# Attention's first score and softmax units placed between the query projections of a two-block kernel

## The reference, cut to what matters

```python
z = rmsnorm(h, g_mix) @ w_in                       # zq: 512, zkv: 768, zg: 24, zc, zm
kc = gelu((kv[0] blocks of 32, stride 16, + pos) @ w_cmp_k1) @ w_cmp_k2   # 31 compressed keys
vc = gelu((kv[1] blocks + pos) @ w_cmp_v1) @ w_cmp_v2
o_c = softmax(q kc^T * 64**-0.5, causal by block end) @ vc        # compressed branch
o_s = softmax(q ks^T * 64**-0.5, causal) @ vs                     # selected: all 8 blocks here
o_w = softmax(q kw^T * 64**-0.5, causal in 512) @ vw              # window: all 512 keys here
o   = gates[0] * o_c + gates[1] * o_s + gates[2] * o_w            # gates = sigmoid(zg)
y_a = o @ w_o_nsa
c   = causal depthwise convolution of 31 taps over c_val * sigmoid(c_gate), 512 channels
```

## Time and profile before

| | us |
|---|---|
| median of 3 runs (2225.15 to 2229.15) | 2225.91 |
| the profiled execution | 2225.84 |
| its span | 2224.1 |
| PE busy in the span | 2059.4 (93%) |
| DVE, ACT, POOL busy | 934.8, 569.8, 349.7 |
| share of PE in the chain that ended last | 81% |

### The profile page before, as it was taken

The page is one execution under the profiler, slowest core; times in us unless marked ns, Lnnn a source line. Parts: engine busy times, 40 slices in busy tenths (PEclk is TensorE's granted clock), DMA queues, the critical chain, the costliest instruction groups (busy, mean ns, idle before and its releaser), DMA issues.

```text
span 2224.1 us, 23734 instructions
## 1 busy us (share of the span) xinstructions
PE 2059.4 (93%) x9948; PEld 1278.4 (57%) x9948; DVE 934.8 (42%) x1319; ACT 569.8 (26%) x879; POOL 349.7 (16%) x231
## 2 busy tenths in 40 slices
PE   5999999899888898988899889988999999999998
PEld 3888777443424233333324235764687778888877
DVE  3667574310101011111111104777786467777554
ACT  4534313100000000000000003337434343334453
POOL 2212021000000000000000001125533323225440
PEclk8999999899999999999999999998999999999998
DMA  8552116699999999999999992330222322232220
GB/s 284 198 201 102 39 51 253 263 390 419 428 427 427 428 428 428 427 428 428 428 427 427 428 424 106 73 104 10 75 77 80 119 76 94 96 111 70 104 95 38
DMA packets 107178, 529.06 MB, mean 238 GB/s; under 512 B 14925, under 2 KB 43713, under 8 KB 82241
## 3 DMA queue, kind: packets, MB, share of 16 engines
q1 hardware_dynamic: 107073, 527.55, 59.4%
HBM read 525.43 MB, written 2.10 MB: 237 GB/s over the span
## 4 chain that ended last, share of the span: by engine, by line
PE 81%; DVE 6%; DMA 6%; issue 3%; ACT 2%; POOL 1%; SPq 0%; ACTq 0%; DVEq 0%
PE bank L992 21%; PE bank L598 13%; PE bank L599 13%; PE bank L600 13%; PE bank L1043 6%; DMA f<-in_w_gate_dram 5%; PE bank L953 3%; PE bank L966 3%; PE bank L609 2%; DVE f L2338 1%; PE bank L852 1%; PE bank L1234 1%; PE bank L1202 1%; PE bank L798 1%; DVE r L383 1%
## 5 line engine op out<-in xcount | busy, mean ns | idle before, releaser
L992 PE MATMUL bank<-f,high 128*64 128x512 f32 x2048 | 472.0, 607 | 49.8 <-issue 31.5
L390 POOL TENSOR_TENSOR r<-f,r 128x1024 fp32r<-128x1024 f32 (+3 forms) x86 | 231.2, 2708 | 1600.9 <-ACT r L377 1564.6
L598 PE MATMUL bank<-r 128*128 128x512 f32 (+1 forms) x1016 | 404.9, 398 | 15.6 <-DVE r L1935 5.0
L599 PE MATMUL bank<-r 128*128 128x512 f32 (+1 forms) x1016 | 399.5, 393 | 0.0
L600 PE MATMUL bank<-r 128*128 128x512 f32 (+1 forms) x1016 | 398.9, 393 | 0.0
L992 PEld LDWEIGHTS bank<-f,high 128*64 128x64 f32 x2048 | 152.2, 139 | 339.5 <-issue 324.8
L2262 DVE SCALAR_TENSOR_TENSOR f<-bank,low,f 128x512 f32<-128x512 f32 x64 | 48.0, 750 | 507.1 <-PE bank L966 507.1
L1043 PE MATMUL bank<-f,high 128*64 128x512 f32 x1024 | 228.8, 604 | 17.4 <-issue 17.4
L598 PEld LDWEIGHTS bank<-r 128*128 128x128 f32 (+1 forms) x1016 | 191.5, 188 | 70.1 <-issue 19.0
L1413 ACT ACTIVATE high<-bank 128x512 f32<-128x512 f32 (+2 forms) x93 | 51.5, 583 | 676.5 <-PE bank L609 340.7
L599 PEld LDWEIGHTS bank<-r 128*128 128x128 f32 (+1 forms) x1016 | 191.9, 189 | 42.4 <-issue 1.7
(11 more groups left out here) (357 smaller groups left out, 1972.2 us busy)
## 6 DMA issues: line engine op xcount, KB each, us to landing
f<-in_w_down_dram SPq DMA_DIRECT2D x66, 2048.0 KB, 21.4
f<-in_w_up_dram SPq DMA_DIRECT2D x64, 2048.0 KB, 22.0
f<-in_w_gate_dram SPq DMA_DIRECT2D x63, 2048.0 KB, 21.6
f<-in_w_in_dram SPq DMA_DIRECT2D x14, 2048.0 KB, 7.9
f<-in_w_up_dram SPq DMA_DIRECT2D x22, 1024.0 KB, 7.1
high<-in_w_ada_dram SPq DMA_DIRECT2D x32, 512.0 KB, 5.4
f<-in_w_ada_dram SPq DMA_DIRECT2D x4, 2048.0 KB, 17.5
f<-in_w_out_dram SPq DMA_DIRECT2D x4, 2048.0 KB, 8.0
```

The costliest lines, as they stand in the source:

```text
L390: up(g.tensor_tensor(low_part(c)[:, z], whole(c)[:, z], high_part(c)[:, z].bitcast(F32), ALU.subtract), "lo_g", c, i)
L598: pe.matmul(o, wh, xh, start=first, stop=False)
L599: pe.matmul(o, wl, xh, start=False, stop=False)
L992: ins = pe.matmul(o[64 * e:64 * e + 64, :], xsT[p % 2][:, 2 * k + r, 64 * e:64 * e + 64], ws[e](2048 * r + 512 * fc), start=k == 0 and r = ...
```

## The change

**Buffers.** Units 0 and 1 write their scores to `PS_first`, two stretches that the projections have used up: the first lies over the column temporaries `ct` and over `pcs`, the second over the spent rows `kcat`. Units 2 to 7 keep `PS[un % 4]`.

**First part.** On PE the scores of unit 0 follow the second query projection, those of unit 1 the third, those of unit 2 the fourth; `hidden_rows` comes behind them. The turn of banks 2 to 7 starts two projections earlier, so the third and fourth projections go to banks of that turn, 2 and 3. ACT's copies of the queries stand between the exponentials. DVE does 39 taps ahead of the first `scored` (55 before), and 4, 4 and 2 among the first three units.

**Compressed branch.** `hidden_turned` and `second_layer` move into unit 0, `compressed` into unit 1 and `compressed_turned` into unit 2.

**Steady part.** On ACT `exps(un + 2, 0)` and `exps(un + 2, 1)` in step un become `exps(un + 2, 1)`, after `turned(un, 0)`, and `exps(un + 3, 0)`, at the end of the step, ahead of the division of `w_o_nsa` and `high_output`. Taps: none in step 1, as before in 2 to 4, 7 instead of 4 in each of 5 to 7; 42 are left behind attention (41 before).

```diff
+        PS_first = [mem(2560, M + 24704), mem(2560, M + 12928)]
...
+        def scored_at(un):
+            return PS_first[un] if un < 2 else PS[un % 4]
...
             for i in range(4):
                 o = take(("q2", i), "a_z", "q2", i)
                 up(project(o[:, :], Q2, i, U2H, U2L), "pe_z", "q2", i)
                 if i == 0:
                     to_tokens(1, 128)
                     to_tokens(2, 24)
+                else:
+                    if i == 1:
+                        turn["order"], turn["i"] = [2, 3, 4, 5, 6, 7], 0
+                        pe.wait_ge(s["v_z"], val("v_z", "kz", 1))
+                    pe.wait_ge(s["a_z"], val("a_z", "q2", i // 2))
+                    for n in range(3):
+                        scores(i - 1, n)
...
-            pe.wait_ge(s["a_z"], val("a_z", "q2", 3))
-            pe.wait_ge(s["v_z"], val("v_z", "kz", 1))
-            for un in range(2):
-                for n in range(3):
-                    scores(un, n)
             hidden_rows()
-            for n in range(3):
-                scores(2, n)
-            hidden_turned()
-            second_layer()
-            compressed()
             for un in range(8):
                 turned(un, 0)
+                if un == 0:
+                    hidden_turned()
+                    pe.wait_ge(s["a_z"], val("a_z", "q2", 3))
+                if un == 1:
+                    compressed()
                 if un < 5:
                     scores(un + 3, 0)
                 turned(un, 1)
+                if un == 0:
+                    second_layer()
+                if un == 2:
+                    compressed_turned()
                 if un < 5:
                     scores(un + 3, 1)
-                if un == 1:
-                    compressed_turned()
...
+            queries(0)
+            a.wait_ge(s["v_z"], val("v_z", "tk", 2))
+            up(a.activation(flat(GT), flat(GT), ACT.Sigmoid), "a_z", "gt")
+            queries(1)
             exps(0, 0)
+            queries(2)
             exps(0, 1)
+            exps(1, 0)
+            queries(3)
+            exps(1, 1)
+            exps(2, 0)
             a.wait_ge(s["pe_cmp"], val("pe_cmp", "rows"))
             up(a.activation(hrow, bank("cm")[:, 0:256], ACT.Gelu_apprx_tanh), "a_cmp", "rows")
-            exps(1, 0)
-            a.wait_ge(s["pe_cmp"], val("pe_cmp", "hid"))
-            up(copy(HID.rearrange("p h w g n -> p (h w g n)"), bank("cmT")[:, 0:256]), "a_cmp", "hid")
-            exps(1, 1)
             for un in range(8):
                 turned(un, 0)
+                if un == 0:
+                    a.wait_ge(s["pe_cmp"], val("pe_cmp", "hid"))
+                    up(copy(HID.rearrange("p h w g n -> p (h w g n)"), bank("cmT")[:, 0:256]), "a_cmp", "hid")
                 if un < 6:
-                    exps(un + 2, 0)
-                if un == 0:
+                    exps(un + 2, 1)
+                if un == 1:
                     a.wait_ge(s["v_att"], val("v_att", "pcs"))
                     up(a.activation(flat(pcs), flat(pcs), ACT.Exp), "a_att", "pc")
                 turned(un, 1)
-                if un < 6:
-                    exps(un + 2, 1)
-                if un == 1:
+                if un == 2:
                     a.wait_ge(s["pe_att"], val("pe_att", "pcT", 0))
                     up(copy(pcT[:, 0, :], bank("pcT", 0)[:, :]), "a_att", "pcT", 0)
+                if un < 5:
+                    exps(un + 3, 0)
                 if un in (2, 3):
                     a_divide(a, WO2, [2 * un - 4, 2 * un - 3])
...
+            conv_taps(6)
             v_divide(v, Q2)
-            conv_taps(12)
+            conv_taps(4)
             to_tokens(1, VS[:, 1, :, :], 128)
             to_tokens(2, GT, 24)
-            conv_taps(22)
+            conv_taps(8)
...
-            for un in range(2):
+            for un in range(3):
                 for n in range(3):
                     scored(un, n)
                 shifts(un)
+                if un < 2:
+                    conv_taps(4)
+                    weights(un, 0)
+                    weights(un, 1)
+            conv_taps(2)
...
-                if un:
-                    conv_taps(2)
+                if un > 1:
+                    conv_taps(2 if un < 5 else 5)
             low_output(3)
```

68 lines of the change are left out of this document (29 added, 39 removed).

## The result

The changed kernel takes 2247.4 us (median of 4 runs, 2242.76 to 2248.25), against 2225.54 for the kernel before beside it (4 runs, 2225.15 to 2229.15). The ratio is 1.0091, with a 95% interval of 1.0078 to 1.0103: slower by 0.9%. The forecast was 2232.5, in a range of 2219 to 2238. Its sign was right, its size a third of what came, and the time lies above the range.

A forecast was written before the change was run, and what follows sets the result against it. PE was taken as the bound behind attention, with waits and low clock inside attention. The profiled 2225.84 us plus 2.1 for the walk at full clock and 4.6 for low clock gave 2232.5, range 2219 to 2238.

The forecast's parts named there:

- What bounds the kernel: Behind attention PE is the bound and nothing waits; inside attention about 20 us are waits and several more low clock.
- Part 1: Query projections: first scores at 1461.6, a 1.8 us wait for bank 3, fourth projection ending 6.7 us later.
- Part 2: Late load of `w_cmp_v`: PE waits 6.1 us ahead of `hidden_rows`, which ends at 1497.8, 3.3 us late.
- Part 3: Steps 0 and 1: unit 4's scores end at 1520.0, putting the change 8.5 us ahead.
- Part 4: Step 2: bank waits of 1.5 and 2.8 us; it ends at 1537.5, the lead down to 1.1 us.
- Part 5: New loop, step 3 onward: waits for ACT of 4.8, 4.2 and 3.7 us; 2.1 us slower at full clock.
- The clock term: Low clock behind the waits of steps 3 and 4: 2.3 us lost each, 4.6 in all.
- Small terms: Last steps: taps ahead of `low_output(3)`, 0 to 2.3 us, and POOL's scalings beside taps, 0 to 2.6; both taken as 0.
- Rival 1: The new loop's waits come but are broken up, so the clock stays full: 2228 us; chance 0.22.
- Rival 2: Steps 2 to 7 last as before and the 8.5 us lead is kept: faster, 2217.3 us; chance 0.18.
- Rival 3: POOL or VectorE becomes the bound of steps 5 to 7: 2.6 us on top, 2235.1 us; chance 0.10.
- Rival 4: The load doesn't hold PE ahead of `hidden_rows`: no 6.1 us wait, 2230 to 2232 us; chance within the forecast's 0.45.

The follow-up runs named there:

- e4: The changed kernel with unit 1's scores behind the fourth query projection, whose copy stands ahead of unit 1's exponentials: 2239.47 us, ratio 1.0056.
- e6: The changed kernel with the edits of e1 and e4 together: 2224.08 us, ratio 0.9988.
- e9: e8 with unit 5's last score step ahead of the values of unit 1 on PE in step 2: 2216.40 us, ratio 0.9956.
- e7: The changed kernel with `high_output` ahead of the exponentials of unit un + 3 at the end of steps 2 and 4: 2241.33 us, ratio 1.0062.
- e3: The changed kernel with PE repeating the second group's first four transposes 4, 8, 8 and 6 times in steps 2 to 5: 2236.33 us, ratio 1.0043.
- e1: The changed kernel with ACT's order in the steps as in the kernel before, from step 1 on: 2226.65 us, ratio 1.0005.
- e8: e6 with taps moved: 7 instead of 2 ahead of step 0, 4 in step 1, 2 instead of 5 ending steps 5 to 7: 2221.37 us.
- e2: The kernel before with only the changed order of exponentials on ACT, from step 2 on: 2240.60 us, ratio 1.0065.
- e10: e8 with the scores of units 0, 1 and 2 behind the fourth projection and no VectorE score copy behind an exponential: 2222.59 us, ratio 0.9981.
- e0: The changed kernel run once more, without any edit: 2244.97 us, ratio 1.0082.

## Why the prediction was right in its sign and wrong in its size

Starts of after are given here less the 4.83 us of the anchor.

- **What bounds the kernel** (attention's waits and clock; a PE bound behind it): right. Behind attention PE is busy for 625.67 of 641 us, before for 626.22 of 640.
- **Part 1**: right. First scores at 1461.7 (forecast 1461.6), the wait for bank 3 1.61 us (1.8).
- **Part 2**: right. The wait for the load is 6.11 us (6.1), and `hidden_rows` ends at 1497.4 (1497.8). `e4`, which takes away 3.3 us of this wait and the 1.61 for the bank, gains 6.5 us, clock included.
- **Part 3**: right. Unit 4's scores are done at 1519.3 (1520.0), 9.2 us ahead of before (8.5).
- **Part 4**: 3.2 us short. Step 2 ends at 1540.7, not 1537.5. The waits for the bank were near (2.38 and 1.08 us, forecast 1.5 and 2.8); two more, of 1.30 and 1.74 for VectorE, have no length in the forecast. What follows was taken at full clock: the values are rows of 1.97 and 4.54 us where `e6` and `e9` have 1.07 and before 2.38, which alone is 3.1. The bank's waits were in the walk and their clock was not.
- **Part 5**: the mechanism was right and the place in steps 3 and 4 too, ACT's wait for the shift at the end of a step with the bank's copy behind it: 4.8 and 4.2 us forecast, 4.48 and 4.00 measured. The third, forecast at 3.7 for step 5, did not come there: with no scores left to take banks, PE does the 20 transposes of step 5 in one row without a wait (2.40 us at 1580.40). It came in step 6, as 0.72 for ACT and 2.51 for VectorE. **Missed: the second arm.** I followed what PE needs of ACT, and of `high_output` only ACT's 0.6 us. VectorE's `low_output` waits for it, and queued behind it are taps and the copy of the middle step. `e7` prices `high_output`'s place at 4.9 us, clock and 0.5 us of ACT's own arm included.
- **The clock term was the one most mis-sized.** This is the step that failed. Forecast 4.6, in steps 3 and 4; `e3` shows at least 7.4. The low clock lasted 13.7, 10.2, 10.2 and 3.4 us in steps 2, 3, 4 and 6, where I had taken the 6 to 8 us of before, once for each wait of steps 3 and 4, and none for step 2. PE's work in these four stretches is 10.8, 7.9, 9.3 and 3.4 us; if half of it is lost, as the forecast reckoned, that is an estimate of 15.7 us. In steps of nearly 18 us with two or three waits, the clock comes back in between for only 6.8, 6.8 and 10.2 us. The Trainium skill's account of such a loop (TensorE: Matmul & The Clock Gate, section "HAM oscillation — how this bites in real kernels"), that each step pays the cold clock anew, was the nearer guide: it named step after step. The trace agrees in steps 2, 3 and 4, with low stretches of 13.7, 10.2 and 10.2 us, and not in step 5, where the clock was 1.00.
- **Small terms**: `low_output(3)` behind the last taps was taken as 0, at the low end of 0 to 2.3; it is the wait of 1.42 us at 1609.03. POOL's upper bound of 2.6 was rightly left out: a wait of 0.26 us in the last unit. Its eight scalings beside taps took 7.58 us against 7.36, and the four of one group 4.71 in one place and 2.38 in another; so POOL was slowed, to twice its time at the most. The Trainium skill's rule (SBUF — State Buffer, section "SBUF: two separate sides"), one engine blocked while the other holds the port, is neither borne out nor excluded by these means over many short instructions.
- **Rivals.** Rival 1 (full clock) fell by `e3`. Rival 2 (the lead is kept) fell: it was to be decided by the wait in step 3, which was 4.48 and not 1.5. But `e1` is that rival's world, with the loop undone, and even there the lead of 9 us at unit 4 came to 1.5 at the end. Step 2 took 5.8 us of it (waits of 1.30, 0.88 and 2.44, the last for the compressed weights, and values of 4.07 us behind them), and the last steps, with seven taps each, 1.8; `e8` and `e9` brought much of it back. Rival 3 did not come in the changed kernel beyond the small terms above, as step 6's 2.51 us hang on `high_output`; with the loop undone it shows, 1.9 us in `e8`. Rival 4 did not come.

**The miss by steps.** The forecast's 2.1 and 4.6 make +6.7 in the stretch, and 16.8 came. Of the 10.1 us between, 3.2 lie ahead of step 3; step 3 took 17.7 us against 12.6 + 2.3, step 4 17.2 against 12.95 + 2.3, and the rest 24.9 against 22.65. In each of them the low clock costs more than was put down for it, and in step 3 the second arm adds 1.21 us.

**The account of the 22 us of the profiles**: 4.8 ahead of the anchor, 16.8 in the stretch, 1.4 at `low_output(3)`, and all else behind gives 1.0 back. Beside the 16.8 stand 12.5 for the loop's order put alone into the old kernel (`e2`) and 18.3 for taking it out of the new one (`e1`), where it also spoils the lead.

**Open**: the 4.8 us. Of the twelve runs eleven stand 1.7 to 4.5 us behind the profile of before at the anchor, and one 0.2; the changed kernel itself showed 4.8 and 2.6. Much of it arises in one place: between 1319 and 1338 us after and ten of the twelve runs fall back by 1.9 to 3.4 us against before, with a low stretch of the clock of 3.4 us that begins at 1331 to 1333 us, and before, `e3` and `e10` have no low stretch there. `e2`, whose code is that of before up to there, has it, and `e3` and `e10`, whose code is that of the changed kernel, do not; so this part belongs to the execution. The medians are not settled by that: in every run the median lies 1.3 to 4.8 us further above the kernel before than its stretch and all behind it account for (4.8 in after, 2.0 in `e0`, 3.7 in `e2`). Either other executions of before are also later at the anchor than its one profile and shorter in the stretch, or something of this size is in every kernel but that of before. No run tells which, and some 2 to 5 us of the loss so have no shown cause.

## What to carry to other kernels

When an in-order engine is told to wait for the newest result of a step, list all that stands behind the wait, and then for each of these the engines that wait for it in their turn: here one move of four exponentials held a PSUM bank on one arm and a copy on VectorE on the other, and all engines idled round a ring. Price a wait of TensorE at its own length and then for the clock behind it, above all where several come in one step: undoing this loop gave 8.7 us of idle time and 9.6 of slower matmuls. And a saved stall is worth only what the next steps can keep: after each edit look for the wait that ends last now: here a wait of 2.4 us for the compressed weights in step 2, worth 5 us once the loop was clean, of which 2.4 are idle time.

## What the runs showed of the hardware that I had not expected

- **Adding matmuls made the kernel faster.** 104 repeated transposes, placed in waits, gave 7.4 us (`e3`).
- **The same wait can cost its clock or not.** The 64 matmuls of `hidden_rows` behind nearly equal waits, in `e6` and in `e8` (9.82 us behind 2.92 in `e9`, 7.13 behind 2.79 in `e4`):

```profile
1486.62 9.81 PE L1178 MATMUL bank<-f,high 128*64 128x256 f32 x64 [3.05 <-DMA f<-in_w_cmp_v_dram]
```

```profile
1486.18 7.13 PE L1178 MATMUL bank<-f,high 128*64 128x256 f32 x64 [3.03 <-DMA f<-in_w_cmp_v_dram]
```

The rows of 1.72 us in `e8` and `e9` are such a pair too. So some 2 us of `e9`'s gain are clock that no wait of its own accounts for; the medians hold them, but by what rule they come these runs don't say.
- **A stretch repeats to 0.1 us** in two executions (`e0` and after, waits of 4.48 and 4.00 in both), though what lies ahead of it moved by 2.3 us. It is one pair, and where the clock falls out otherwise, as above, a stretch can differ by 2.7 us.
